# A transformer pair on one core: eight chunks of squares summed one by one on TensorE, ahead of the second projection of each layer

## The reference, cut to what matters

```python
def _rms_norm(x, gain):
    xf = x.astype(jnp.float32)
    y = xf * lax.rsqrt(jnp.mean(xf * xf, axis=-1, keepdims=True) + NORM_EPS)
    return (y * gain.astype(jnp.float32)).astype(x.dtype)

for l in range(DEPTH_2):
    h = _rms_norm(x, attn_norm[l])
    proj = h @ w_in[l]
    ...
```

## Time and profile before

| What | Value |
|---|---|
| Median of 3 runs | 1664.33 us (1659.05 to 1666.41) |
| The profiled execution, its own time | 1668.98 us |
| Its span, first to last instruction | 1667.20 us |
| Mean granted TensorE clock | 0.988 of full speed |
| Busy: PE, PEld, DVE, ACT, POOL | 96%, 88%, 53%, 55%, 72% |
| Layer 0 and layer 1 begin at about | 1011 us and 1337 us |

### The profile page before, as it was taken

One profiled execution on the slowest core, in us unless ns is written; L12 is line 12 of the kernel. 1 busy time (PEld: TensorE's weight loads), 2 busy tenths in 40 slices (PEclk: granted clock), 3 DMA queues, 4 the chain that ended last, 5 costly groups with the idle time before them and its releaser, 6 DMA issues.

```text
span 1667.2 us, 32057 instructions
## 1 busy us (share of the span) xinstructions
PE 1604.0 (96%) x12800; PEld 1467.8 (88%) x12800; DVE 887.5 (53%) x1817; ACT 920.5 (55%) x1551; POOL 1194.2 (72%) x500
## 2 busy tenths in 40 slices
PE   8988999999999999999999999989999998999998
PEld 7876999999999998888888888768999996789997
DVE  6988445994366667777611115777220077762101
ACT  6666665445444445555566666376553364766533
POOL 5652777998878877777888888215888870269885
PEclk9999999999999999999999999999999999999999
DMA  7341555666555555555666665523666554146663
GB/s 259 128 137 39 169 185 176 191 193 190 189 177 178 176 172 173 176 176 169 195 190 193 193 194 165 178 75 102 192 188 190 184 172 165 54 138 209 195 192 112
DMA packets 79891, 280.42 MB, mean 168 GB/s; under 512 B 8704, under 2 KB 9472, under 8 KB 79488
## 3 DMA queue, kind: packets, MB, share of 16 engines
q1 hardware_dynamic: 79744, 278.38, 53.3%
HBM read 277.30 MB, written 1.05 MB: 167 GB/s over the span
## 4 chain that ended last, share of the span: by engine, by line
PE 85%; DVE 6%; ACT 3%; issue 3%; POOL 1%; DMA 1%; DVEq 0%; SPq 0%; ACTq 0%; POOLq 0%
PE ps L2687 14%; PE ps L2048 13%; PE ps L2356 11%; PE ps L2665 7%; PE ps L2694 7%; PE ps L2666 7%; PE ps L2670 7%; PE ps L552 6%; POOL wl L213 1%; PE ps L2651 1%; PE ps L2653 1%; PE ps L386 1%; PE ps L2182 1%; DMA slots<-w 1%; PE ps L2096 1%
## 5 line engine op out<-in xcount | busy, mean ns | idle before, releaser
L2465 POOL TENSOR_TENSOR wl<-slots,wh 128x1024 fp32r<-128x1024 f32 x256 | 619.3, 2421 | 124.9 <-ACT wh L2403 122.8
L213 POOL TENSOR_TENSOR wl<-slots,wh 128x1024 fp32r<-128x1024 f32 x178 | 430.1, 2421 | 300.5 <-ACT wh L199 299.5
L2403 ACT ACTIVATE wh<-slots 128x1024 fp32r<-128x1024 f32 x256 | 272.4, 1064 | 350.4 <-issue 228.5
L199 ACT ACTIVATE wh<-slots 128x1024 fp32r<-128x1024 f32 x178 | 188.8, 1062 | 168.2 <-PE ps L2356 65.9
L2665 PE MATMUL ps<-xh,wh 128*128 128x256 f32 x1024 | 241.9, 279 | 0.0
L2666 PE MATMUL ps<-xl,wh 128*128 128x256 f32 x1024 | 238.9, 276 | 0.0
L2665 PEld LDWEIGHTS ps<-xh,wh 128*128 128x128 f32 x1024 | 192.3, 188 | 0.1
L2666 PEld LDWEIGHTS ps<-xl,wh 128*128 128x128 f32 x1024 | 192.3, 188 | 0.0
L213 POOL TENSOR_TENSOR third_lo<-slots,third_hi 128x1024 fp32r<-128x1024 f32 x58 | 141.3, 2436 | 31.1 <-ACT third_hi L199 31.1
L2687 PE MATMUL ps<-wh,xh 128*128 128x512 f32 x508 | 160.1, 396 | 0.0
L2687 PE MATMUL ps<-wh,xl 128*128 128x512 f32 x508 | 158.0, 392 | 0.0
(11 more groups left out here) (430 smaller groups left out, 3433.5 us busy)
## 6 DMA issues: line engine op xcount, KB each, us to landing
slots<-w SPq DMA_DIRECT2D x260, 512.0 KB, 3.8
slots<-wu SPq DMA_DIRECT2D x128, 512.0 KB, 3.6
slots<-wv SPq DMA_DIRECT2D x128, 512.0 KB, 3.5
arena<-bias SPq DMA_DIRECT2D x1, 2048.0 KB, 8.0
h<-xT SPq DMA_DIRECT2D x4, 256.0 KB, 5.9
arena<-keys SPq DMA_DIRECT2D x1, 1024.0 KB, 7.7
yT<-y_out SPq DMA_DIRECT2D x2, 512.0 KB, 2.8
layer<-consts SPq DMA_DIRECT2D x1, 800.0 KB, 5.3
```

What stands on the lines that cost most here:

```text
L199: act.activation(self.hi[self.place[n]], self.slots[:, u % SLOTS, :], ACT.Copy).then_inc(self.rounded, 1)
L213: pool.tensor_tensor(self.lo[self.place[n]], self.slots[:, self.order[n] % SLOTS, :], self.hi[self.place[n]].bitcast(F32), ALU.subtract).t ...
L2403: act.activation(whv[:, r % 2, :], slots_v[:, r % SLOTS, :], ACT.Copy).then_inc(w_hi, 1)
L2465: pool.tensor_tensor(wlv[:, r % 2, :], slots_v[:, r % SLOTS, :], whv[:, r % 2, :].bitcast(F32), ALU.subtract).then_inc(w_lo, 1)
```

## The change

In each of the two layers VectorE's two calls of `add_squares` for the first norm are gone, and TensorE sums the eight chunks of `sq` itself, by eight products with the matrix of ones in full f32. They stand ahead of "ckr" and no longer between its halves; ahead of every second one TensorE waits for the pair of squares. The four other calls of `add_squares` per layer stay; the values of `l_pre` that their sums wait for are counted anew.

```diff
@@ layers_dve
-                for half in range(2):
-                    dve.wait_ge(h_sq, 8 * l + 2 * half + 2)
-                    add_squares(dve, sq[:, 4 * half:4 * half + 4, :], half, l_pre)
                 banks.wait_drained(dve, ("ms", l))
                 link(dve.reciprocal(rst[:, 0:T], std[:, 0:T]))
@@ layers_pe
                 split_pair(("cq", l), 2 * l)
-                split_pair(("ckr", l), between=lambda: sums(("ms", l), (0, 1), added, ready=(l_pre, 6 * l + 2)))
+
+                def stage_sums():
+                    bank = banks.open(pe, ("ms", l))
+                    for c in range(DC):
+                        if c % 2 == 0:
+                            pe.wait_ge(h_sq, 8 * l + c // 2 + 1)
+                        ins = pe.matmul(bank[:, 0:T], const("ones"), sq[:, c, :], start=(c == 0), stop=(c == DC - 1))
+                    banks.close(ins, ("ms", l))
+
+                stage_sums()
+                split_pair(("ckr", l))
                 split_pair(("q", l, 0))
...
-                        sums(("mn", l), (0,), added, ready=(l_pre, 6 * l + 3))
+                        sums(("mn", l), (0,), added, ready=(l_pre, 4 * l + 1))
...
-                        sums(("mm", l), (1,), added, ready=(l_pre, 6 * l + 4))
+                        sums(("mm", l), (1,), added, ready=(l_pre, 4 * l + 2))
...
-                        sums(("mf", l), range(2), added, ready=(l_pre, 6 * l + 6))
+                        sums(("mf", l), range(2), added, ready=(l_pre, 4 * l + 4))
```

## The result

The kernel with the change takes 1668.53 us in the median of 20 runs (1662.48 to 1674.21), the kernel before, in 20 runs, 1664.16 us (1659.05 to 1666.41). The ratio is 1.0029, 95% interval 1.0019 to 1.0040: 4.4 us slower by the medians, and within 0.5%. In a second measurement beside its variants it was 1.0030 (1.0019 to 1.0042).

A forecast was written before the change was run, and what follows sets the result against it. TensorE was taken to bound the kernel; 2.61 us in layer 1 plus 1.97 in layer 0 gave +4.6 us, 1668.9 us on the median (1673.6 for the profiled execution), range 1666 to 1672, within 0.5%.

The forecast's parts named there:

- The price of a sum: First norm on TensorE, per layer: eight f32 sums take 3.47 us instead of 0.86 for two, net 2.61 us.
- No wait for the squares: Ahead of "ckr": the squarings end 0.44 and 0.91 us before its present start, so TensorE's earlier wait costs 0.
- VectorE worth nothing: First norm: removing VectorE's reductions of 4.08 and 4.02 us gains 0 on the path, since idle time follows them.
- Layer 0, less what its wait hides: Layer 0's "ckr": the wait for third_lo goes and hides part of the added sums, leaving +1.97 us.
- Layer 1: Layer 1's first norm and projections: nothing to hide the added sums behind, so +2.61 us.
- pace: "ckr" and q0: fp32r products run at two paces; effect taken as 0, bounds -0.2 to +0.6 us.
- The rival that they swallow both shifts: Weight transfers at L2217, if not released by TensorE, absorb the extra TensorE time: 1664.3 us, chance 0.09.
- that pace as something the change might flip: Feed-forwards: layer 0 turns fast, 1662.5 us, chance 0.14; or layer 1 turns slow, 1675.3 us, chance 0.13.
- if the long stretches change pace: Sign that the prediction is wrong: the feed-forward streams change pace in the changed profile; 6.38 us between the layers before.

The follow-up runs named there:

- the two sums above: The changed kernel with only two of the eight chunks summed, still ahead of the second projection, no reductions on VectorE: 1666.71 us, 1.0008 of the kernel before.

## Why the prediction was right

*The price of a sum.* I took 3.47 us for eight, from the loop at the kernel's end; measured are 3.45 us in both layers, 216 ns a record. The Trainium skill, "TensorE: Matmul & The Clock Gate", section "Back-to-back issue gap", gives N/2.4 + 2.5 ns for an isolated product and names no data type. An estimate by that, 109 ns for each of the 16 records, would have been 1.75 us.

*No wait for the squares.* This was right: between the last squaring and the first sum 0.35 and 0.62 us were left.

*VectorE worth nothing.* This was right, and putting the reductions back shows it.

*Layer 0, less what its wait hides.* The forecast was 1.97 us, and 2.00 to 2.10 are measured against the three profiles of before; the wait for third_lo is gone as forecast.

*Layer 1.* The forecast was 2.61 us, and 2.69 to 2.90 are measured. The sums alone are 2.59 (3.45 - 0.86); the rest is pace, since all 96 products behind them came at the slow one (11.31 us against 2.82 + 8.18 in the first profile of before). That is +0.31 us, which I had taken as 0 and as 0.28 at worst.

*The transfers further down.* The rival that they swallow both shifts did not come: in all eleven traces the chain goes from TensorE into them, with nothing but SyncE's issue between. From the last product of "cq" to the end of that transfer, layer 1 has 49.02 to 49.71 us in the three profiles of before, and 52.13 and 52.51 us in the two of the change. Layer 0 has 51.09 to 51.32 us before, and 51.70 and 53.15 us after: in the first profile of the change a shorter transfer took back most of the shift there, in the second next to none of it.

*Sum.* The forecast was 4.6 us and 1668.9 us, and 4.4 us and 1668.53 us are measured. That they lie within 0.4 us of each other is partly luck: the parts of the table add up to 4.7 to 5.0 us, and the interval of the ratio spans 3.2 to 6.7 us.

*One number was wrong.* I took the profiled execution as typical of the kernel and forecast 1673.6 us for the profile after it; that took 1667.60. The step that failed is the one from the profile to the median. The profile lay 4.65 us above the median and had a feed-forward slower by 6.38 us, and I had listed that pace as something the change might flip, with 0.14 and 0.13, instead of as something that this one execution had. The profile had the sign in it: two layers with the same code, one of them slower than the other. My own list of signs had "if the long stretches change pace" as one of being wrong, and between the two first profiles layer 0's did; two more executions of the kernel before show that it was not the change that did it.

## What to carry to other kernels

Work moved from an idle engine's slack to an engine that is the path costs its length there, less what a wait behind it gives back (here 2.6 us a layer, and about 2.1 in layer 0); the first question is what the chain does behind the work that goes, not how long it is. Price a product by the records of the same type and shape: for 128x256, f32 takes two records at 216 ns where fp32r takes one at 113 to 118. A sum over partitions by ones can be had in fp32r, if the squares may be rounded to it. Before two profiles are compared, compare stretches that the change can't touch; here 6.4 us of difference in them hid a loss of 5.

## What the runs showed of the hardware that was not expected

**Two paces.** In these traces a stream of fp32r products of 128x256 runs at 113.3 or at 117.8 ns from start to start, with the granted clock at 1.00 over both, and keeps its pace through hundreds of products and through changes of weights, of line and of PSUM bank (1510 in a row in the first profile of before). It changed at breaks: short waits, or sums. Behind the 16 records of the eight sums it was slow in both layers of every run that has them; behind two f32 sums in the same place it was fast (10.90 us for 96 in the chain of the two sums above). In the attention's projections it alternates from one to the next, 5.46 and 5.65 us for 48. What in a break decides it stays open; the traces don't show it.

**A multiplication of 2.62 or 0.41 us.** These are VectorE's two products with the reciprocal root in layer 1, with GpSimd's subtractions beside them, first two fences from the kernel before and then two from after the change:

```profile
1352.12 1.77 DVE L1808 TENSOR_TENSOR ps<-layer,rst 128x256 f32<-128x256 f32 x1
1353.80 2.62 DVE L1809 TENSOR_TENSOR attention<-layer,rst 128x256 f32<-128x256 f32 x1
```

```profile
1351.17 4.97 POOL L213 TENSOR_TENSOR wl<-slots,wh 128x1024 fp32r<-128x1024 f32 x2
```

```profile
1349.95 0.45 DVE L1805 TENSOR_TENSOR ps<-layer,rst 128x256 f32<-128x256 f32 x1
1350.32 0.41 DVE L1806 TENSOR_TENSOR attention<-layer,rst 128x256 f32<-128x256 f32 x1
```

```profile
1347.71 2.40 POOL L213 TENSOR_TENSOR wl<-slots,wh 128x1024 fp32r<-128x1024 f32 x1 [1.10 <-ACT wh L199]
1350.54 2.45 POOL L213 TENSOR_TENSOR wl<-slots,wh 128x1024 fp32r<-128x1024 f32 x1 [0.42 <-ACT wh L199]
```

Before, the two took 4.39 us beside GpSimd's subtractions, and each ended 0.29 us behind the end of one (at 1353.89 behind 1353.60, where the first of the row's two ends, and at 1356.43 behind 1356.14). After the change they started at the end of one and in the gap of 0.42 us ahead of the next, and took 0.86. The Trainium skill, "SBUF — State Buffer", section "SBUF: two separate sides", says that VectorE and GpSimd share a pair of ports, that a VectorE instruction with two inputs in SBUF needs it while a GpSimd instruction reads SBUF, and that whichever of the two starts first keeps it for its whole length and blocks the other. These rows agree with it, with VectorE as the one that is blocked: 2.62 us instead of 0.41. In layer 0 the changed kernel's second product still takes 2.62 us, so the gain is a matter of where the products fall. Nobody waited for the two products in either kernel, so it is not part of the result.
